# Rwkv slots of twelve steps: another placing of the features, the norm and the readout

## The chip, the cores and the metric

The kernel runs on one core of one Trainium2 chip. The metric is the device time of one execution in microseconds. The kernel before takes 4650.03 us (median of three runs, 4646.21 to 4650.68).

## The reference

Two transformer-like blocks of depth 2 run one after the other on 512 tokens of width 1024 (with 256 context tokens). Nearly all of it is left alone here. The change lies in the rwkv mixer of the first block: features are made from the projected keys, a decay and a rate; a linear recurrence over the tokens runs in both directions; and the outcome is normalised, gated and projected.

```python
kk = kk * lax.rsqrt(jnp.maximum(jnp.sum(kk * kk, axis=-1, keepdims=True), 1e-24))
decay = jnp.exp(-jnp.exp(-jax.nn.softplus(-w_raw) - 0.5))
a = jax.nn.sigmoid(heads(a0[d] + (xa @ a1[d]) @ a2[d]))
k_d = kh * (1 + (a - 1) * k_a_h)
...
S = (S * w_t[:, :, None, :]
     - jnp.einsum('bhij,bhj->bhi', S, kk_t)[..., None] * kka_t[:, :, None, :]
     + v_t[..., None] * k_t[:, :, None, :])
...
yn = ((y - mean) * lax.rsqrt(var + GN_EPS)).reshape(B, L, D_MODEL) * ln_g + ln_b
bonus = (jnp.sum(r * k_sum * r_k.astype(jnp.float32), axis=-1, keepdims=True) * v).reshape(B, L, D_MODEL)
return ((yn + bonus) * g).astype(dtype) @ wo
```

## The kernel before

Every engine runs its own instruction list. Each of these lists is made by the same Python walk, `rwkv_steps`, which calls `prep`, `scan`, `feature` and `readout` of that engine in one order. An engine does its list strictly in that order and waits on semaphores. So the tables that the change touches set the order in all five lists at once.

The sixteen heads are worked on as eight pairs. The 768 tokens of a pair are 12 chunks of 64, in three groups of four chunks, and each group of a pair is one slot: 24 slots in all, of 12 steps each (`PREP_STEPS`), t = 0 to 23. Slot t prepares its group in both directions (d = 0 and 1), and beside it the recurrence `scan` of the group of slot t - 1 runs, one part at every step: four chunks by three parts.

The preparation inverts a triangular matrix by levels. Step 0 makes the small and the big grams (PE L1722, L1732; the masked copy L3526 on VectorE and the products with a mask L3536 or L3538). Steps 2 to 9 are four levels of two steps: at an even step PE makes a product (L1782) and VectorE copies it under a mask (`copy_predicated`, L3544); at the odd step PE makes two (L1795, L1799) and ScalarE copies both (L2418). Step 10 is PE L1786 and the two ScalarE copies L2425, step 11 is PE L1810 and the two VectorE copies L3552. Each of these waits for the one before, and the two directions take turns. GpSimd sets the target of each masked copy to the unit matrix ahead of it (L1144).

`scan` has a product from the state (PE L1823) and VectorE L3570 in part 0, PE L1833 and the ScalarE copies L2439 in part 1, and PE L1845, L1852 and L1857 with VectorE L3577, L3579 and L3585 or L3589 in part 2.

The features of the *next* pair are made in the slots of this one, by `FEATURES[t % 3]`: a step's features are issued behind that step's `prep` and `scan`. `norm` of the pair *after* that is placed by `NORM_AHEAD` in the third slot. The readout of the pair *before* stands in the second slot by `READOUT` (not changed), its parts `turn` and `bonus` by `AHEAD` in the third. What each issues:

- lora: PE L1866 and ScalarE L2461 (Sigmoid), two each. recip: VectorE L3601, 128 columns of six. kk: L3603. run: a scan on VectorE, L3609. rate_k: ScalarE L2465 (Identity). key and rate: VectorE L3613, L3615.
- exp(d,0) and exp(d,1): ScalarE L2472, L2474 (Exp). exp(1,0) waits for kr(0,2), and kr(d,...) for exp(d,0). kr: VectorE L3624 to L3634; k_sum: L3637; bk: L3648; bonus: L3639.
- square: ScalarE L2449. norm: PE L1873 and VectorE L3596. root: ScalarE L2453 (Sqrt), behind norm.
- readout: centre (PE L1879), squares (ScalarE L2485), var (PE L1892, VectorE L3667), root (ScalarE L2488, Sqrt), recip0 to recip3 (VectorE L3673), scale, shift (L3676, L3679), gate (PE L1895, VectorE L3683), turn (PE L1884, ScalarE L2482), bonus (PE L1888, VectorE L3663).

Sigmoid, Exp and Sqrt each want their own table on ScalarE; a load stands in the list wherever one of them follows another. Copy, Identity and Square go with any. Two PSUM banks are used in turn by the small grams, the turned blocks, lora, norm and the readout (`misc_banks`), in the order of this same walk.

Of the kernel before, what the change touches and what calls it, by code (L numbers as in the profile page):

```python
# [294 lines left out]
def build_program(nc, panels, vecs, consts, x_in, c_in, mem_in, pool_w, bias, pos, window_in, out, x_save):  # L295
    npanels = panels.shape[0]
    with ExitStack() as ctx:
        def sb(name, shape, dt=F32):
            return ctx.enter_context(nc.sbuf_tensor(name, shape, dt))
# [13 lines left out]
        square = sb("square", [P, 2, TOK])  # L313
# [9 lines left out]
        def area(at, *shape):  # L323
            n = int(np.prod(shape))
            flat = arena[:, at:at + n]
            if len(shape) == 1:
                return flat
            names = " ".join("abcd"[:len(shape)])
            return flat.rearrange(f"p ({names}) -> p {names}", **{"abcd"[i]: s for i, s in enumerate(shape)})
# [297 lines left out]
        k_sum = area(RING0 + LORA_SLOT * PANEL + 3 * D, LAT)  # L627
# [15 lines left out]
        bk = [area(Y0 + d * 2 * BLOCK, CHUNKS // 2, 4, C) for d in range(2)]  # L643
# [116 lines left out]
        def ys(group):  # L760
# [6 lines left out]
        SCAN_AT = tuple(range(PREP_STEPS))  # L767
        RECIPS = 6
        FEATURES = (
            {0: [("recip", 0, 0)], 1: [("recip", 0, 1)], 2: [("recip", 0, 2)], 3: [("recip", 0, 3), ("lora", 0, 0)],  # L770
             4: [("recip", 0, 4)], 5: [("lora", 1, 0), ("recip", 0, 5)], 6: [("kk", 0, 0)], 7: [("run", 0, 0)],
             8: [("run", 0, 1)], 9: [("lora", 0, 1), ("run", 0, 2)], 10: [("lora", 1, 1), ("run", 1, 0)]},
            {0: [("run", 1, 1)], 1: [("rate_k", 0, 0), ("run", 1, 2)], 2: [("key", 0, 0)],
             3: [("rate_k", 1, 0), ("rate", 0, 0)], 5: [("exp", 0, 0)], 7: [("exp", 0, 1)]},
            {0: [("kr", 0, 0)], 1: [("kr", 0, 1), ("kr", 0, 2), ("exp", 1, 0)], 2: [("key", 1, 0)], 3: [("rate", 1, 0), ("exp", 1, 1)],
             4: [("kr", 1, 0)], 5: [("kr", 1, 1), ("kr", 1, 2), ("k_sum", 0, 0)], 6: [("bk", 0, 0)], 7: [("bk", 0, 1)],
             8: [("bk", 1, 0)], 9: [("bk", 1, 1)], 10: [("bonus", 0, 0)]})
        NORM_AHEAD = {9: "square", 10: "norm", 11: "root"}
        EARLY = [("square", 0, 0), ("norm", 0, 0), ("root", 0, 0), ("lora", 0, 0), ("lora", 1, 0), ("lora", 0, 1), ("lora", 1, 1)]
        EARLY += [("recip", 0, i) for i in range(RECIPS)] + [("rate_k", 0, 0), ("rate_k", 1, 0), ("kk", 0, 0)]  # L780
        EARLY += [("run", d, i) for d in range(2) for i in range(3)] + [("exp", 0, 0), ("exp", 0, 1)]
# [1 line left out]
        LATE = [("kr", 0, 0), ("kr", 0, 1), ("kr", 0, 2), ("bk", 0, 0), ("bk", 0, 1), ("exp", 1, 0), ("exp", 1, 1), ("kr", 1, 0), ("kr", 1, 1),  # L783
                ("kr", 1, 2), ("bk", 1, 0), ("bk", 1, 1), ("bonus", 0, 0)]

        AHEAD = {9: "turn", 10: "bonus"}
        READOUT = {1: ("centre",), 3: ("squares",), 4: ("var",), 5: ("root",), 6: ("recip0",), 7: ("recip1",), 8: ("recip2",),
                   9: ("recip3",), 10: ("scale", "shift"), 11: ("gate",)}

        def rwkv_steps(e):  # L790
# [9 lines left out]
            for t in range(groups + 1):  # L800
                for k in range(PREP_STEPS):
# [9 lines left out]
                    for what, d, i in FEATURES[t % GROUPS].get(k, ()):  # L811
                        if t // GROUPS + 1 < PAIRS:
                            e["feature"](t // GROUPS + 1, what, d, i)
                    if t % GROUPS == 2 and k in NORM_AHEAD and t // GROUPS + 2 < PAIRS:
                        e["feature"](t // GROUPS + 2, NORM_AHEAD[k], 0, 0)
                    if t % GROUPS == 1 and t > GROUPS and k in READOUT:
                        for what in READOUT[k]:
                            e["readout"](t // GROUPS - 1, what)
                    if t % GROUPS == 2 and k in AHEAD:
                        e["readout"](t // GROUPS, AHEAD[k])  # L820
            for k in sorted(READOUT):
# [3001 lines left out]
```

## Time and profile before

| | before |
|---|---|
| median of three runs | 4650.03 us |
| lowest, highest | 4646.21, 4650.68 us |
| the profiled execution | 4651.23 us, its span 4649.4 us |
| granted TensorE clock, mean | 0.974 |
| rwkv loop | about 1338 to 2000 us of the span |

The page gives the busy time of each engine over the whole span; the table of stretches gives it for a stretch, with the granted clock as a share of 2.4 GHz. A timeline row is the start, the length, the engine, the line and the operation, and in brackets the time that the engine sat idle before it with what ended that.

### The profile page before, as it was taken

To read this page: it belongs to the slowest core of one execution; us is meant where nothing else is said; L and a number is where in the kernel's file an instruction comes from. 1 tells how busy PE (TensorE), PEld (TensorE's weight loads), DVE (VectorE), ACT (ScalarE), POOL (GpSimd) and SP (SyncE) were. 2 spreads that over 40 slices of the span, in tenths; PEclk is the share of its full clock that TensorE was granted. 3 is DMA by queue.
4 is the path that set the end of the run, shared out by engine and by line. 5 is a ranking of instruction groups with operands and counts; after the bars stand their busy time and mean duration, and the time that the engine had idled before them with its cause. 6 is when DMAs were issued, how large, how long until landed. Compare 5 with 4: busy or idle time off the path is not lost.

```text
span 4649.4 us, 75968 instructions
## 1 busy us (share of the span) xinstructions
PE 4431.9 (95%) x32488; PEld 3163.7 (68%) x32488; DVE 2738.7 (59%) x4988; ACT 1042.5 (22%) x2236; POOL 243.0 (5%) x317
## 2 busy tenths in 40 slices
PE   8999999999988888899999999989999999989998
PEld 4555555556456666668886888547886888546887
DVE  3164545536358777645565666665657666674657
ACT  1053000012046666530002110341001010251000
POOL 0001000001001112110000000300000000110000
PEclk9999999999999999999999999989999999989999
DMA  5310222211200000122222222211222222201221
GB/s 210 146 63 37 91 109 109 109 55 57 84 2 3 4 4 4 39 83 73 91 91 76 90 74 82 91 37 73 91 86 86 77 86 82 91 37 73 91 91 46
DMA packets 27071, 339.45 MB, mean 73 GB/s; under 512 B 3025, under 2 KB 3025, under 8 KB 6897
## 3 DMA queue, kind: packets, MB, share of 16 engines
q1 hardware_dynamic: 24048, 324.51, 18.4%
q0 software_dynamic: 2688, 10.09, 0.6%
q8 instruction: 258, 4.23, 0.4%
q14 instruction: 77, 0.62, 0.0%
HBM read 330.40 MB, written 4.19 MB: 72 GB/s over the span
## 4 chain that ended last, share of the span: by engine, by line
PE 86%; DVE 8%; ACT 3%; issue 2%; DMA 1%; SPq 0%; DVEq 0%; ACTq 0%
PE ps L1583 47%; PE ps L1200 20%; PE ps L1209 2%; PE ps L1732 1%; PE ps L1795 1%; PE ps L1354 1%; PE ps L1253 1%; PE ps L1799 1%; PE ps L1516 1%; PE ps L1845 1%; ACT arena L2171 1%; PE ps L1866 1%; DVE arena L3536 1%; DMA arena<-in_panels 1%; PE ps L1662 1%
## 5 line engine op out<-in xcount | busy, mean ns | idle before, releaser
L1583 PE MATMUL ps<-arena 128*128 128x256 f32 (+1 forms) x9096 | 2108.6, 394 | 15.6 <-DVE arena L3199 15.6
L1583 PEld LDWEIGHTS ps<-arena 128*128 128x128 f32 x9096 | 1729.6, 190 | 381.7 <-DVE arena L3199 18.0
L1200 PE MATMUL ps<-arena 128*128 128x512 f32 (+3 forms) x2816 | 997.9, 515 | 0.4 <-DVE arena L2780 0.4
L1200 PEld LDWEIGHTS ps<-arena 128*128 128x128 f32 x2816 | 524.2, 190 | 460.1 <-issue 396.7
L3190 DVE TENSOR_TENSOR arena<-ps,arena 128x512 f32<-128x512 f32 (+1 forms) x250 | 157.6, 630 | 306.4 <-PE ps L1583 304.5
L3190 DVE TENSOR_TENSOR square<-ps,square 128x512 f32<-128x512 f32 (+1 forms) x145 | 99.1, 684 | 176.1 <-PE ps L1583 176.0
L3131 DVE TENSOR_TENSOR arena<-arena 128x1024 f32<-128x1024 f32 (+2 forms) x153 | 190.5, 1245 | 3.3
L2342 ACT COPY square<-ps 128x512 f32<-128x512 f32 (+1 forms) x65 | 37.2, 573 | 655.8 <-PE ps L1583 583.1
L1077 POOL TENSOR_TENSOR arena<-arena 128x512 f32<-128x512 f32 x60 | 72.0, 1200 | 1473.2 <-ACT arena L2142 1466.6
L2342 ACT COPY arena<-ps 128x384 f32<-128x384 f32 (+1 forms) x35 | 18.6, 530 | 572.3 <-PE ps L1583 546.5
L2418 ACT COPY arena<-ps 128x512 f32<-128x512 f32 x192 | 112.1, 585 | 99.7 <-PE ps L1799 95.6
L1144 POOL COPY square<-const 128x256 f32<-128x256 f32 x144 | 90.8, 638 | 725.4 <-PE ps L1799 497.0
L3199 DVE TENSOR_TENSOR arena<-arena 128x1024 f32<-128x1024 f32 (+1 forms) x60 | 72.4, 1207 | 87.2 <-ACT square L2342 78.4
L2171 ACT ACTIVATE arena<-arena,state_sum 128x256 f32<-128x256 f32 (+2 forms) x128 | 76.5, 598 | 207.0 <-DVE state_sum L2760 204.7
L3190 DVE TENSOR_TENSOR reset<-ps,square 128x512 f32<-128x512 f32 (+1 forms) x65 | 43.9, 675 | 132.7 <-PE ps L1583 132.7
L1583 PE MATMUL ps<-arena,square 128*128 128x256 f32 (+1 forms) x432 | 122.0, 431 | 0.0
L1209 PE MATMUL ps<-arena 128*128 128x256 f32 (+1 forms) x336 | 106.2, 478 | 15.1 <-DVE arena L2965 8.4
L1782 PE MATMUL ps<-arena 64*64 64x64 f32 x3072 | 91.3, 230 | 25.9 <-ACT arena L2418 20.3
L2333 ACT ACTIVATE reset<-arena 128x256 f32<-128x256 f32 x40 | 16.7, 417 | 422.7 <-DVE arena L3264 422.7
L3186 DVE TENSOR_TENSOR arena<-arena 128x1024 f32<-128x1024 f32 (+2 forms) x100 | 107.6, 1076 | 3.4
L3205 DVE TENSOR_TENSOR arena<-arena 128x1024 f32<-128x1024 f32 (+2 forms) x100 | 107.0, 1070 | 1.1
L1583 PEld LDWEIGHTS ps<-arena,square 128*128 128x128 f32 x432 | 82.1, 190 | 33.3
(392 smaller groups left out, 5201.1 us busy)
## 6 DMA issues: line engine op xcount, KB each, us to landing
arena<-in_panels SPq DMA_DIRECT2D x144, 2048.0 KB, 7.8
arena<-in_panels SPq DMA_DIRECT2D x9, 1536.0 KB, 6.4
arena<-in_bias POOLq DMA_DIRECT2D x8, 512.0 KB, 4.3
arena<-in_x_in SPq DMA_DIRECT2D x1, 3072.0 KB, 10.9
x_save<-arena POOLq DMA_DIRECT2D x1, 2048.0 KB, 7.5
arena<-x_save POOLq DMA_DIRECT2D x1, 2048.0 KB, 14.1
out_x<-arena SPq DMA_DIRECT2D x8, 256.0 KB, 2.9
arena<-in_panels SPq DMA_DIRECT2D x1, 1792.0 KB, 11.7
```

The costliest lines, as they stand in the source:

```text
L1144: pool.tensor_copy(step_sb[d][level % 2], unit).then_inc(sem("step_unit"), one("step_unit"))
L1200: ins = pe.matmul(dest, left(k), right(k), start=(k == 0), stop=(k == nk - 1))
L1209: ins = pe.matmul(bank[:, 0:b - a], w[:, k, m * P:(m + 1) * P], src[:, k, a:b], start=(k == 0), stop=(k == KD - 1))
L1583: ins = pe.matmul(bank[:, j * cut.side:(j + 1) * cut.side], left[:, k, j * P:(j + 1) * P], right[k], start=(k == 0), stop=(k == cut.rows - 1))
L1782: ins = pe.matmul(ps[half(home(level, h, pos)), 2 * d + pos, q * C:(q + 1) * C], left[half(pos), :], right[half(pos), :], start=True, stop ...
L2171: act.activation(p_h, p_h, ACT.Exp, bias=soft_at(i, h, NEGMAX), scale=-1.0, accum_out=soft_at(i, h, SUM)).then_inc(sem(f"exped{h}"), one(f ...
L2418: act.copy(both_sb[par][d], both_banks(d)[:, :, P:3 * P].rearrange("p a (w x) -> p a w x", w=2)).then_inc(sem(f"x_ready{d}"), one(f"x_read ...
L3131: ins = dve.tensor_tensor(part, x[:, rows], y[:, rows], op)
L3186: dve.tensor_tensor(a21, left_block(w, 0, 0, c), a21, ALU.subtract).then_inc(sem("left"), one("left"))
L3190: dve.tensor_tensor(out, product_of(tile(), cut), other, ALU.add).then_inc(sem("tile_free"), one("tile_free"))
L3199: dve.tensor_tensor(a11, left_block(total, 0, 0, cut), a11, ALU.subtract).then_inc(sem("tile_free"), one("tile_free"))
L3205: dve.tensor_tensor(a12, a12, a11, ALU.subtract).then_inc(sem("left"), one("left"))
```

## The change

Three tables change; no instruction is added, taken away or made otherwise, except the table loads, which follow the order of ScalarE's functions.

- First slot of a pair: recips 3 to 5 and kk at steps 4 and 6, lora(0,1) and lora(1,1) at steps 7 and 9 (were 9 and 10), run by run one step earlier or later.
- Second slot: rate from step 3 to 4, rate_k(1) from 3 to 9, exp(0,0) from 5 to 7, exp(0,1) from 7 to 9.
- Third slot: exp(1,0) from step 1 to 3, exp(1,1) from 3 to 5, k_sum from 5 to 6. Square, norm and root from steps 9, 10, 11 to 7, 8, 9. The readout's turn from 9 to 5, its bonus from 10 to 11.

```diff
         FEATURES = (
-            {0: [("recip", 0, 0)], 1: [("recip", 0, 1)], 2: [("recip", 0, 2)], 3: [("recip", 0, 3), ("lora", 0, 0)],
-             4: [("recip", 0, 4)], 5: [("lora", 1, 0), ("recip", 0, 5)], 6: [("kk", 0, 0)], 7: [("run", 0, 0)],
-             8: [("run", 0, 1)], 9: [("lora", 0, 1), ("run", 0, 2)], 10: [("lora", 1, 1), ("run", 1, 0)]},
-            {0: [("run", 1, 1)], 1: [("rate_k", 0, 0), ("run", 1, 2)], 2: [("key", 0, 0)],
-             3: [("rate_k", 1, 0), ("rate", 0, 0)], 5: [("exp", 0, 0)], 7: [("exp", 0, 1)]},
-            {0: [("kr", 0, 0)], 1: [("kr", 0, 1), ("kr", 0, 2), ("exp", 1, 0)], 2: [("key", 1, 0)], 3: [("rate", 1, 0), ("exp", 1, 1)],
-             4: [("kr", 1, 0)], 5: [("kr", 1, 1), ("kr", 1, 2), ("k_sum", 0, 0)], 6: [("bk", 0, 0)], 7: [("bk", 0, 1)],
+            {0: [("recip", 0, 0)], 1: [("recip", 0, 1)], 2: [("recip", 0, 2)], 3: [("lora", 0, 0)],
+             4: [("recip", 0, 3), ("recip", 0, 4)], 5: [("lora", 1, 0)], 6: [("recip", 0, 5), ("kk", 0, 0)], 7: [("lora", 0, 1)],
+             8: [("run", 0, 0), ("run", 0, 1)], 9: [("lora", 1, 1), ("run", 0, 2)], 10: [("run", 1, 0)]},
+            {0: [("run", 1, 1)], 1: [("rate_k", 0, 0), ("run", 1, 2)], 2: [("key", 0, 0)], 4: [("rate", 0, 0)],
+             7: [("exp", 0, 0)], 9: [("exp", 0, 1), ("rate_k", 1, 0)]},
+            {0: [("kr", 0, 0)], 1: [("kr", 0, 1), ("kr", 0, 2)], 2: [("key", 1, 0)], 3: [("exp", 1, 0), ("rate", 1, 0)],
+             4: [("kr", 1, 0)], 5: [("exp", 1, 1), ("kr", 1, 1), ("kr", 1, 2)], 6: [("k_sum", 0, 0), ("bk", 0, 0)], 7: [("bk", 0, 1)],
              8: [("bk", 1, 0)], 9: [("bk", 1, 1)], 10: [("bonus", 0, 0)]})
-        NORM_AHEAD = {9: "square", 10: "norm", 11: "root"}
+        NORM_AHEAD = {7: "square", 8: "norm", 9: "root"}
...
-        AHEAD = {9: "turn", 10: "bonus"}
+        AHEAD = {5: "turn", 11: "bonus"}
         READOUT = {1: ("centre",), 3: ("squares",), 4: ("var",), 5: ("root",), 6: ("recip0",), 7: ("recip1",), 8: ("recip2",),
                    9: ("recip3",), 10: ("scale", "shift"), 11: ("gate",)}
```

## Rows read from the trace of the kernel before

**Rows 1.** The page: busy time, share of the span and instructions of an engine.

```profile
PE 4431.9 (95%) x32488; PEld 3163.7 (68%) x32488; DVE 2738.7 (59%) x4988; ACT 1042.5 (22%) x2236; POOL 243.0 (5%) x317
```

**Rows 2.** The table of stretches: slots 10, 11, 12 and 22 of the loop.

```profile
core 0: us, PE busy (x) PEld busy (x) DVE busy (x) ACT busy (x) POOL busy (x), PEclk, DMA share, GB/s
...
1612.00:1643.80 31.80, 25.37 (x662) 18.65 (x662) 21.46 (x46) 22.47 (x46) 3.89 (x8) 0.87 0.01 3
1643.80:1671.40 27.60, 24.92 (x736) 19.93 (x736) 24.01 (x59) 15.80 (x36) 6.80 (x8) 0.96 0.02 4
1671.40:1696.40 25.00, 23.13 (x722) 18.08 (x722) 18.93 (x43) 17.21 (x41) 4.69 (x8) 1.00 0.01 3
...
1944.00:1974.40 30.40, 26.77 (x674) 20.06 (x674) 18.41 (x41) 15.65 (x38) 3.22 (x8) 0.85 0.01 3
```

**Rows 3.** Groups of ScalarE by line, 1338 to 2000: busy us, mean ns, idle before.

```profile
L2488 ACT ACT_TABLE_LOAD x7 | 9.0, 1283 | 0.1
L2474 ACT ACT_TABLE_LOAD x6 | 7.7, 1283 | 0.1
```

**Rows 4.** Timeline of ScalarE, slot 10: start, length, line, operation.

```profile
1623.78 1.03 ACT L2465 ACTIVATE arena<-arena,omka,vec 128x768 f32<-128x768 f32 x1
...
1628.81 1.28 ACT L2472 ACT_TABLE_LOAD   x1
1630.11 0.84 ACT L2472 ACTIVATE arena<-arena 128x768 f32<-128x768 f32 x1
1630.97 1.28 ACT L2488 ACT_TABLE_LOAD   x1
1632.26 0.63 ACT L2488 ACTIVATE rstd<-rstd 128x512 f32<-128x512 f32 x1
1632.80 0.57 ACT L2418 COPY arena<-ps 128x512 f32<-128x512 f32 x1
```

**Rows 5.** Timeline of TensorE, slot 10; in brackets its idle time before.

```profile
1625.38 1.13 PE L1892 MATMUL ps<-square,const 128*128 128x512 f32 x2 [0.98 <-ACT square L2485]
...
1633.42 0.46 PE L1782 MATMUL ps<-arena 64*64 64x64 f32 x16 [2.77 <-ACT arena L2418]
...
1640.55 2.08 PE L1895 MATMUL ps<-arena 128*128 128x512 f32 x2
```

**Rows 6.** The table of stretches, four us each, from slot 10 into 11.

```profile
1630.00:1634.00 4.00, 1.13 (x50) 0.85 (x50) 1.04 (x2) 3.92 (x8) 0.68 (x2) 1.00 0.00 0
1634.00:1638.00 4.00, 3.49 (x118) 3.04 (x120) 3.90 (x8) 3.40 (x5) 0.77 (x2) 0.72 0.02 4
...
1642.00:1646.00 4.00, 4.00 (x41) 3.10 (x41) 1.39 (x3) 0.37 (x1) 0.00 (x0) 0.50 0.00 0
1646.00:1650.00 4.00, 3.86 (x100) 3.13 (x99) 3.74 (x9) 1.73 (x6) 0.00 (x0) 1.00 0.02 4
```

**Rows 7.** Timeline of TensorE, slots 11 and 12.

```profile
1665.87 1.87 PE L1873 MATMUL ps<-square,const 128*128 128x384 f32 x4
...
1668.55 0.44 PE L1810 MATMUL ps<-arena 32*32 32x32 f32 x16
...
1691.17 0.92 PE L1866 MATMUL ps<-arena 64*128 64x384 f32 x4
```

**Rows 8.** Timeline of ScalarE, end of slot 11.

```profile
1666.73 0.53 ACT L2425 COPY arena<-ps 32x128 f32<-32x128 f32 x2
...
1668.38 1.28 ACT L2453 ACT_TABLE_LOAD   x1
```

**Rows 9.** Timeline of VectorE, slot 11, steps 5 to 8.

```profile
1658.74 0.68 DVE L3637 TENSOR_TENSOR arena<-arena 128x512 f32<-128x512 f32 x1
...
1662.27 0.43 DVE L3544 COPY_PREDICATED square<-const,ps 128x256 f32<-128x256 int32 x1
```

**Rows 10.** Timeline of TensorE, slot 22, which has a readout and no features.

```profile
1971.76 1.12 PE L1895 MATMUL ps<-arena 128*128 128x512 f32 x2
```

## What was predicted

> **What bounds the kernel now.** I read the page first. TensorE (PE) is busy 95% of the span and ScalarE (ACT) 22% [rows 1], but that is a mean over unlike stages. The change touches only the rwkv loop, about 1338 to 2000 us, so I cut that loop into its slots, taking the first masked copy of a slot (L3526) as its start. The table of stretches shows four slots of one kind each: a second slot of a pair with readout (31.8 us), a third (27.6), a first (25.0), and the last second slot, which has a readout but no features of a next pair (30.4) [rows 2]. No engine is full in the long one: PE 25.4, DVE 21.5, ACT 22.5 of 31.8 us [rows 2]. What sets its length is a ring: a product on PE, a masked copy on VectorE (DVE, L3544), a product, a copy on ACT (L2418), with the second direction half a step behind. A feature costs only what it adds to the queue ahead of the next ring instruction on its engine. So I follow each queue, in order of time, for one pair (slots 10, 11 and 12).
>
> **Second slot of a pair (31.8 us now).** Three ScalarE pieces stand in the ring.
> - Step 3: the rate_k activation (1.03 us) stands ahead of the readout's squares [rows 4], and PE waits 0.98 us for these before it starts the variance sum L1892 [rows 5]. The new table moves rate_k of direction 1 to step 9. PE is then free some 0.15 us before the squares end: 0.8 us won.
> - Step 5: a table load and exp(0,0), then another load and the readout's root, stand between two ring copies, from 1628.81 to 1632.89 [rows 4]; PE's next product waits 2.77 us [rows 5]. exp(0,0) goes to step 7, so 1.28 + 0.84 = 2.1 us leave this place. The recip pieces behind the root start as much earlier. In all L2418 would start near 1629.9 instead of 1632.80: 2.9 won.
> - Step 7: exp(0,0) with its load, 2.1 us, replaces exp(0,1), which has a load too [rows 3] and works on as many elements: nothing.
> - Step 9: exp(0,1) (0.84) and rate_k (1.03) now stand between the last L2418 and the first L2425, 1.9 us where nothing stood. PE has only its two small L1786 products and one L1833 to do meanwhile, and then waits about 1.8 us. Given back: 1.4 (the rest is the 0.3 to 0.5 us that L2425 was late anyway).
> - The variance read and rate on DVE: rate moves from step 3 to 4, into a wait; nothing.
> - The gate product L1895 takes 2.08 us here [rows 5] and 1.12 in the slot without features [rows 10]: the granted clock falls between 1634 and 1638, is 0.50 (1.2 GHz) until 1646 and then full again [rows 6]. With full clock the products of steps 9 to 11 win some 1.5 us together.
> Sum: -2.9 + 1.4 - 1.5 = **-3.0 us** if the clock stays full, -1.5 if it is half again by the gate product.
> The loads: L2488 and L2474 have their own load in each such slot [rows 3]; one of three loads goes in six slots, 6 x 1.28 = 7.7 us of ScalarE time. That is already in the 2.1 above. The Trainium skill (ScalarE: Activation LUTs, "What ACT_TABLE_LOAD costs") counts about 2.66 us for each switch, a drain included, and asks to group by set; here a load begins 0.02 us after the activation before it ends (1630.95) and its own activation follows 0.01 us behind it [rows 4], so no drain is to be seen and the sum goes by 1.28. By the page's figure the six would be 16 us.
>
> **Third slot (27.6 us now).**
> - k_sum (0.68 us) leaves step 5, where it holds up the masked copies of step 6 [rows 9], but stands at step 6 with bk(0,0), and bk(0,1) follows at step 7 as before. The copy of step 8, at 1662.27 [rows 9], comes when all of them are done, as now. Won at step 6, lost at step 8: 0.
> - exp(1,0) and exp(1,1) go to steps 3 and 5, each into a gap of ScalarE: 0. The turn (four transposes and a copy) at step 5 also falls in waits.
> - norm: four products L1873, 1.87 us [rows 7], move from step 10 to 8, ahead of L1795 of step 9. DVE releases the second direction's product only some 1.3 us later than the first's, so part is covered: +1.5.
> - root: load 1.28 + 0.84 = 2.1 us goes from step 11 [rows 8], where it hid under PE's queue, to step 9, ahead of L2425. The two squares and the turn's copy that stood there (1.7 us) leave: +0.4.
> - Step 10: the norm and bonus products that PE had there kept L1810 back to 1668.55 [rows 7], 1.3 us past the end of the copies it needs (L2425, 1667.26 [rows 8]); that goes: -1.3. But the copies L2439 and the second L2425 that this covered now follow in the open: +0.4.
> - The readout's bonus product L1888 at step 11 (about 1.05 us, by the like product L1895 at full clock [rows 10]) stands right ahead of the next slot: +1.05.
> Sum: **+2.1 us** (bounds +1.0, if the norm products hide behind the DVE queue, to +2.9, if nothing is covered).
>
> **First slot (25.0 us now).** The recips 3 to 5 and kk move between gaps of DVE; at most 0.2. The lora pair that ran at step 10, where ScalarE's copies covered most of it, now goes to step 7, ahead of L1782 of step 8: four L1866, 0.92 us [rows 7]. **+0.65 us** (bounds +0.2 and +0.9).
>
> **The rest.** Seventh first slot +0.65; slot 1, which has no readout to separate exp from exp, gets the 1.9 us of step 9: +1.5; slots 20 and 23 get the bonus at step 11: +0.5 each. Together +3.2.
>
> **The clock.** In the pair that I follow it falls once: in 1630 to 1634 PE is busy 1.13 of 4 us, and then the clock is 0.50 for some 10 us [rows 6]. The new table takes that hole away, but opens two others, of 1.8 us at step 10 of the second slot and of 2.1 us at step 10 of the third, with hardly any product around them: by my walk PE is busy some 1.2 of 3.5 us in each. That is about the share after which it fell [rows 6]. Right behind each hole comes the densest stretch, the gate or bonus product and the first products of the next slot, which is bound by PE. Half clock over some 3.5 us there costs about 1.5 us each time, by 2.08 against 1.12 for one product [rows 5, 10]. As the second slot's own end at half clock is the present state, the first costs back the 1.5 counted above; the second comes on top.
> The likeliest sum, for six pairs: 6 x (-3.0 + 2.1 + 0.65 + 1.5 + 1.5) = 6 x 2.75 = 16.5, and with the rest 19.7. Since the half clock may spare a seam now and then I take 18. The profiled execution is 4651.2 us (span 4649.4), 1.2 above the median of 4650.0, so 4650 + 18 = **4668 us**.
>
> **Rivals.**
> - **It is faster: the clock stays full.** Mechanism: the hole behind ScalarE's pair of loads (2.77 us) was the cause, and holes of about 2 us at step 10 don't suffice. Then the third slot also starts at full clock, which saves 1.1 us more, and if the norm products hide as well (+1.0): 6 x (-3.0 - 1.1 + 1.0 + 0.65) + 3.2 = -11.5: 4638. With norm as walked: 6 x (-1.35) + 3.2 = -5: 4645. It decides at a PE wait at step 10 of under about 1 us. For it: in the slot without features the same steps have no hole and stay at full clock. Against: 1.9 and 2.1 us of ScalarE work stand there without cover.
> - **Half clock at one of the two seams**, 6 x 1.25 + 3.2 = +11: 4661; if the other gains run 0.5 us better for each pair, +8: 4658.
> - **Half clock for longer than one such stretch.** Now it lasts about 10 us, not 3.5; two of these in a pair cost another 1 us each: +30: 4680.
> - **The change does nothing**: ring waits absorb the moves, the table load saved is not on the path: 4650. Against: the 2.77 us wait ends with that copy [rows 5].
>
> **Chances.** Forecast (both seams) 0.33, longer half clock 0.11, one seam 0.2 (0.09 of it above 0.2%), full clock 0.3 (0.2 of it below 4640.7, as the other terms of the walk have room on that side too), nothing 0.06. About 0.2%, 9.3 us, is what a measurement of this kernel can tell from no change. So faster 0.2, slower 0.33 + 0.11 + 0.09 = 0.53, same the rest, 0.27. The range takes in the full-clock case with its low bound and the longer half clock: 4636 to 4684.
>
> **What would show it.** Six loads fewer in all (L2474 without any). L2418 of step 7 some 2.9 us earlier in second slots. PE waits of 1.5 to 2.2 us for L2425 at step 10 of second and third slots. Second slots near 28.7 to 30.2 us, third ones near 29.7 to 31, first ones 25.7 (27 with half clock). The granted clock at 0.50 around the starts of slots and no longer before them. Wrong if the third slot is no longer than now: then the norm and root moves are covered by something that I don't see.

## The result, and the profile after

The changed kernel takes 4692.81 us (median, 4678.03 to 4694.34), the kernel before 4648.12 us beside it: a ratio of 1.0091 with the 95% interval 1.0068 to 1.0114. The forecast had the side (slower) and two of the three places where the clock falls, but it said 4668 us and a range up to 4684: the loss is more than twice what it gave.

The page after, engines and clock, to be laid beside [rows 1]:

```profile
PE 4463.4 (95%) x32488; PEld 3187.3 (68%) x32488; DVE 2740.2 (58%) x4988; ACT 1036.7 (22%) x2230; POOL 222.8 (5%) x317
...
PEclk9999999999998888899999999989999999989999
```

TensorE is busy 31.5 us longer with the same 32488 products, and five slices of the clock's line, those of the rwkv loop, have gone from 9 to 8. ScalarE issues six instructions fewer: the six table loads. The span is 4691.6 us, 42.2 more than before. The table of stretches, first for the whole loop and then for the slots 10, 11, 12 and 22 (as [rows 2]; columns as there):

```profile
1343.90:2019.30 675.40, 588.01 (x15942) 453.76 (x15941) 469.84 (x1071) 400.53 (x892) 92.26 (x184) 0.87 0.03 9
...
1633.60:1665.70 32.10, 26.82 (x660) 19.75 (x662) 21.43 (x45) 20.49 (x44) 3.30 (x8) 0.82 0.01 3
1665.70:1696.10 30.40, 26.42 (x728) 20.43 (x728) 23.84 (x59) 17.47 (x39) 5.05 (x8) 0.89 0.01 4
1696.10:1725.90 29.80, 27.11 (x726) 21.55 (x728) 19.41 (x44) 16.57 (x38) 3.85 (x8) 0.84 0.01 3
1991.40:2019.30 27.90, 24.13 (x660) 17.17 (x661) 18.53 (x41) 15.87 (x39) 3.20 (x8) 0.94 0.01 3
```

and the same loop, 23 slot lengths, in the kernel before:

```profile
1343.20:1974.40 631.20, 553.15 (x15956) 428.75 (x15953) 468.82 (x1071) 406.31 (x898) 112.36 (x184) 0.93 0.03 10
```

The loop has grown by 44.2 us, which is all of the loss. VectorE's busy time is the same (468.8 and 469.8), ScalarE's is less (406.3 and 400.5). What grew is TensorE's, by 35 us, and its clock went from 0.93 to 0.87. A share of 0.87 over 675.4 us is 2 x 0.13 x 675.4 = 176 us at half clock, against 2 x 0.07 x 631.2 = 88 us before. So there are 88 us more at half clock and 44 us more of time. This quotient, a half, is no price yet, as it also holds what the queues gained and lost; the first experiment gives about 0.4 us of time for each microsecond at half clock. Slot 22, with no features in it, is 2.5 us shorter than before, at a clock of 0.94 instead of 0.85.

The second slot is as long as before (32.1 against 31.8), the third is 2.8 us longer, the first 4.8 us. The two waits that the forecast spoke of, on TensorE (timeline; the idle time before it in brackets), slots 10 and 11:

```profile
1660.66 0.51 PE L1810 MATMUL ps<-arena 32*32 32x32 f32 x16 [1.84 <-ACT arena L2425]
...
1661.84 0.64 PE L1810 MATMUL ps<-arena 32*32 32x32 f32 x16
1662.41 2.08 PE L1895 MATMUL ps<-arena 128*128 128x512 f32 x2
...
1665.46 2.08 PE L1732 MATMUL ps<-arena 64*128 64x128 f32 x16
...
1690.51 0.44 PE L1810 MATMUL ps<-arena 32*32 32x32 f32 x16 [2.25 <-ACT arena L2425]
...
1692.32 0.64 PE L1810 MATMUL ps<-arena 32*32 32x32 f32 x16
1692.88 2.08 PE L1888 MATMUL ps<-arena,const 128*128 128x512 f32 x2
...
1695.94 1.97 PE L1732 MATMUL ps<-arena 64*128 64x64 f32 x16
```

And what ScalarE did meanwhile:

```profile
1658.30 0.85 ACT L2474 ACTIVATE arena<-arena 128x768 f32<-128x768 f32 x1
1659.04 1.02 ACT L2465 ACTIVATE arena<-arena,omka,vec 128x768 f32<-128x768 f32 x1
1660.08 0.53 ACT L2425 COPY arena<-ps 32x128 f32<-32x128 f32 x2
...
1687.77 1.28 ACT L2453 ACT_TABLE_LOAD   x1
1689.07 0.84 ACT L2453 ACTIVATE rstd<-rstd 128x768 f32<-128x768 f32 x1
1689.93 0.53 ACT L2425 COPY arena<-ps 32x128 f32<-32x128 f32 x2
```

The two waits are there, of 1.84 and 2.25 us (walked, that is, followed queue by queue in the prediction: 1.8 and 2.1), each ended by L2425 behind two pieces of ScalarE work. Right behind each the products run at half speed: L1895 and L1888 take 2.08 us instead of 1.12 [rows 10]. The clock over these stretches:

```profile
1658.40:1661.00 2.60, 0.76 (x40) 0.58 (x36) 2.13 (x3) 2.53 (x7) 0.00 (x0) 0.98 0.02 6
1661.00:1665.00 4.00, 3.95 (x43) 2.13 (x40) 2.21 (x7) 2.89 (x9) 0.00 (x0) 0.50 0.00 0
1665.00:1668.50 3.50, 3.50 (x53) 3.09 (x50) 1.56 (x4) 0.00 (x0) 0.00 (x0) 0.61 0.00 0
...
1688.00:1692.00 4.00, 1.63 (x55) 1.33 (x56) 2.03 (x6) 3.44 (x8) 0.00 (x0) 0.95 0.00 0
1692.00:1696.00 4.00, 4.00 (x44) 2.20 (x40) 1.81 (x5) 2.23 (x6) 0.00 (x0) 0.50 0.02 4
1696.00:1700.00 4.00, 4.00 (x48) 3.77 (x48) 1.89 (x5) 0.00 (x0) 0.00 (x0) 0.50 0.00 0
1700.00:1704.00 4.00, 4.00 (x67) 3.11 (x69) 2.57 (x4) 1.53 (x5) 0.00 (x0) 0.50 0.00 0
1704.00:1708.00 4.00, 4.00 (x114) 3.29 (x113) 2.43 (x6) 1.60 (x4) 0.03 (x1) 0.84 0.02 4
...
1722.00:1726.00 4.00, 2.93 (x90) 2.40 (x88) 2.28 (x8) 3.47 (x12) 0.00 (x0) 0.97 0.00 0
1726.00:1730.00 4.00, 2.47 (x30) 2.18 (x30) 1.74 (x4) 1.07 (x3) 0.00 (x0) 0.50 0.01 4
1730.00:1734.00 4.00, 4.00 (x60) 3.25 (x56) 1.93 (x4) 0.76 (x3) 0.00 (x0) 0.68 0.00 0
```

The clock falls at the end of the second slot, of the third, and of the first one too (in what follows, at three seams): about 7, 13.5 and 7 us of half clock, 27 in a pair, where it was about 10 [rows 6]. In the third slot's case it lasts through the whole dense start of the next slot. The experiments ask whether the clock is the cause or only goes with it.

### The profile page after: what moved, and what is told of

The parts are those of the page before. It is cut to its first block, busy times and chain, and to the rows that moved or that the text cites. A ratio compares the mean times of both kernels' runs of the same rounds, so it can differ in the third digit from the quotient of the medians.

```text
span 4691.6 us, 75966 instructions
## 1 busy us (share of the span) xinstructions
PE 4463.4 (95%) x32488; PEld 3187.3 (68%) x32488; DVE 2740.2 (58%) x4988; ACT 1036.7 (22%) x2230; POOL 222.8 (5%) x317
## 4 chain that ended last, share of the span: by engine, by line
PE 86%; DVE 7%; ACT 4%; issue 2%; DMA 1%; SPq 0%; DVEq 0%; ACTq 0%
PE ps L1583 46%; PE ps L1200 20%; PE ps L1209 2%; PE ps L1732 2%; PE ps L1354 1%; PE ps L1795 1%; PE ps L1253 1%; PE ps L1722 1%; ACT arena L2171 1%; PE ps L1516 1%; PE ps L1845 1%; PE ps L1799 1%; ACT arena L2418 1%; DVE arena L3536 1%; DMA arena<-in_panels 1%
## 5 line engine op out<-in xcount | busy, mean ns | idle before, releaser
L2418 ACT COPY arena<-ps 128x512 f32<-128x512 f32 x192 | 111.7, 584 | 82.8 <-PE ps L1799 77.5
L1144 POOL COPY square<-const 128x256 f32<-128x256 f32 x144 | 75.5, 526 | 791.0 <-PE ps L1799 562.0
L1583 PEld LDWEIGHTS ps<-arena,square 128*128 128x128 f32 x432 | 82.1, 190 | 33.3
L2705 DVE SCALAR_TENSOR_TENSOR arena<-arena,vec 128x512 f32<-128x512 f32 x120 | 103.4, 902 | 1.3
```

Of the source, the lines that this page charges most:

```text
L1144: pool.tensor_copy(step_sb[d][level % 2], unit).then_inc(sem("step_unit"), one("step_unit"))
L1583: ins = pe.matmul(bank[:, j * cut.side:(j + 1) * cut.side], left[:, k, j * P:(j + 1) * P], right[k], start=(k == 0), stop=(k == cut.rows - 1))
L2418: act.copy(both_sb[par][d], both_banks(d)[:, :, P:3 * P].rearrange("p a (w x) -> p a w x", w=2)).then_inc(sem(f"x_ready{d}"), one(f"x_read ...
L2705: ins = dve.scalar_tensor_tensor(conv_y[:, c, :], src, w, conv_y[:, c, :], ALU.mult, ALU.add)
```

## Experiments

**Does the clock carry the loss?** The changed kernel, with products on TensorE that nobody reads, put into its waits at the start of step 11. They go to the PSUM bank that is free there, behind the wait that frees it.

```diff
+                elif k in (11,) and d == 0:
+                    b = len(plan) % 2
+                    plan[("hold", t, k)] = (4 + b, last[b])
...
+                if k in (11,) and d == 0:
+                    bank = misc("hold", t, k)
+                    for _ in range(8):
+                        pe.matmul(ps[:, bank, 0:P], ident, ident, start=True, stop=True)
```

> The changed kernel with eight products of 128 columns that nobody reads put on TensorE at the start of step 11 of every slot, where it sits waiting (about 1.4 us of work in waits of 1.8 to 2.2 us); nothing else differs. Theory 1 (the granted clock, which falls after the waits at step 10, carries most of the loss): the clock is at 0.50 for under 5 us in a pair instead of 27, the three slots take 28.7, 29.7 and 25.8 us instead of 32.0, 30.5 and 29.8, and the kernel 4645 us (4637 to 4655). Theory 2 (the loss is the longer queues of ScalarE and VectorE and the norm products themselves): the slots stay within 0.3 us of the changed kernel's or grow, 4690 to 4700 us.

Measured: 4642.54 us, ratio to the kernel before 0.9992 (0.9982 to 1.0001), 50 us less than the changed kernel by doing more work. The slots of one pair (second, third, first) take 28.0, 27.6 and 26.5 us. The end of slot 10, TensorE's timeline, and then the loop and the stretch around that seam:

```profile
1632.84 2.05 PE L1720 MATMUL ps<-const 128*128 128x128 f32 x16
1634.82 0.44 PE L1817 MATMUL ps<-arena 32*32 32x32 f32 x16
1635.31 0.45 PE L1852 MATMUL ps<-arena 128*64 128x64 f32 x8
1635.85 0.44 PE L1817 MATMUL ps<-arena 32*32 32x32 f32 x16
1636.22 1.12 PE L1902 MATMUL ps<-arena 128*128 128x512 f32 x2
```

```profile
1344.90:1965.80 620.90, 563.72 (x16312) 446.18 (x16310) 468.09 (x1070) 400.41 (x892) 93.23 (x184) 0.99 0.03 10
...
1634.00:1638.00 4.00, 3.86 (x68) 2.62 (x68) 3.03 (x8) 3.82 (x13) 0.00 (x0) 1.00 0.00 0
```

(Its lines are 7 further down: L1902 is the gate product, L1817 is L1810.) The fillers take 2.05 us, not the 1.4 that the expectation gave, so they stick out a little, and the first slot pays 0.8 us for them; yet the gate product is back at 1.12 us and the loop is at full clock, 0.99. Theory 2, the queues alone, is out: all ScalarE and VectorE queues are as in the changed kernel, and the loss is gone. The three slots take 82.1 us together instead of 92.3, with none of the 27 us of half clock left: 10.2 / 27, or 0.38 us for each, and 0.41 if the 0.8 us of the fillers is counted in.

Half as many fillers:

> The changed kernel with four unread products at step 11 instead of eight (0.7 us of work in waits of 1.8 to 2.2). If the clock falls after a stretch with too little work in it, four are near the bound: it stays full at some seams and falls at others, half clock 5 to 15 us in a pair, 4650 to 4670 us. If each product only hides in its wait and the clock is no matter: 4692.

4640.71 us, 0.9990 (0.9981 to 0.9999). Better than expected. The clock holds behind nearly all second slots and falls for 3 to 7 us behind most third ones, some 33 us in the loop. Four (about 1 us) buy nearly as much clock as eight and cost the first slot less (25.9 us).

Is it that they fill the *wait*, or would products anywhere do? The same eight at step 3:

> The changed kernel with the same eight unread products, but at the start of step 3 of every slot, where TensorE does not wait long; the waits of step 10 stay open. Theory 1 (the clock falls because of the thin stretch at steps 10 and 11, so the place matters): the clock falls as in the changed kernel, about 170 us of half clock in the loop, and the products add 1.0 to 1.4 us to each of 24 slots: 4715 to 4730 us. Theory 2 (more products anywhere raise the mean activity and keep the clock up): under 60 us of half clock, 4650 to 4680.

```diff
-                elif k in (11,) and d == 0:
+                elif k in (3,) and d == 0:
...
-                if k in (11,) and d == 0:
+                if k in (3,) and d == 0:
```

4721.87 us, 1.0161 (1.0144 to 1.0178): in the expected band, 29 us above the changed kernel. The clock over its loop is 0.91, some 126 us of half clock (expected: 170, and 176 without the products). So the place decides most of it: at step 11 the same eight leave next to nothing of the half clock, at step 3 they take away some 50 us, which theory 1 had not foreseen, and cost more than that brings.

**The same in the kernel before.** Its own fall came behind the 2.77 us wait of step 8 [rows 5, 6].

```diff
+                elif k in (8,) and d == 0 and t % GROUPS == 1:
+                    b = len(plan) % 2
+                    plan[("hold", t, k)] = (4 + b, last[b])
...
+                if k in (8,) and d == 0 and g == 1:
+                    bank = misc("hold", t, k)
+                    for _ in range(12):
+                        pe.matmul(ps[:, bank, 0:P], ident, ident, start=True, stop=True)
```

> The kernel before with twelve products of 128 columns that nobody reads on TensorE at the start of step 8 of every second slot, in the wait of 2.77 us there. Theory 1 (clock): it no longer falls in the second slot; second slot 30.1 us, third 26.6: 4631 us (4624 to 4638). Theory 2 (queues alone): 4647, or longer by what sticks out of the wait.

4639.88 us, 0.9989 (0.9980 to 0.9998). The direction is as theory 1 has it, the size is not: 7 us, not 16. The clock over the loop is 0.97 instead of 0.93, so some 50 us less at half clock, and the loop is 8.9 us shorter: under 0.2 us for each here. The second slot is 30.5 us. Twelve products are over 3 us long by the 2.05 for eight, more than the wait, and TensorE also waits in that slot for other reasons; how much of the missing gain is which was not measured.

**Which part of the change makes the waits?** Each of the kernel before with one part.

Second slot's table alone:

```diff
-             3: [("rate_k", 1, 0), ("rate", 0, 0)], 5: [("exp", 0, 0)], 7: [("exp", 0, 1)]},
+            {0: [("run", 1, 1)], 1: [("rate_k", 0, 0), ("run", 1, 2)], 2: [("key", 0, 0)], 4: [("rate", 0, 0)],
+             7: [("exp", 0, 0)], 9: [("exp", 0, 1), ("rate_k", 1, 0)]},
```

> The kernel before with only the second slot's table changed (exp at steps 7 and 9, rate_k at 9, rate at 4). Theory 1 (clock): the 2.8 us wait of step 7 goes and one of about 1.9 us at step 10 comes, the clock still falls once in a pair, later and for some 7 us; second slot 29.7 us, third 27.6: 4637 us (4630 to 4645). Theory 2 (queues alone): 2.9 us less and 1.4 more, 1.5 in each pair: 4641. If the seam behind it gets longer than now: 4650.

4640.51 us, 0.9985 (0.9976 to 0.9994), second slot 29.7 us: faster, as both theories said, which differ too little here to be told apart.

First slot's table alone:

```diff
-             8: [("run", 0, 1)], 9: [("lora", 0, 1), ("run", 0, 2)], 10: [("lora", 1, 1), ("run", 1, 0)]},
+             8: [("run", 0, 0), ("run", 0, 1)], 9: [("lora", 1, 1), ("run", 0, 2)], 10: [("run", 1, 0)]},
```

(with the lora and recip moves of steps 3 to 7 as in the change)

> The kernel before with only the first slot's table changed (the last lora pair from steps 9 and 10 to 7 and 9, recips by two). Theory 1 (clock): without the lora products at step 10 the stretch at the end of the first slot is thin, the clock falls in some pairs and the second slot starts 2.3 us longer: first slot 25.7, kernel 4662 us (4654 to 4672). Theory 2 (queues alone): 0.6 us in each pair: 4653 to 4655.

4656.92 us, 1.0015 (1.0006 to 1.0025). The first slot is 25.7 us, 0.6 more, and the second behind it 32.7 instead of 31.7, as the clock falls at the end of the first. That is 10 us from a table whose own queues cost 4: theory 1.

The norm part alone:

```diff
-        NORM_AHEAD = {9: "square", 10: "norm", 11: "root"}
+        NORM_AHEAD = {7: "square", 8: "norm", 9: "root"}
```

> The kernel before with only square, norm and root put at steps 7, 8, 9 of the third slot. Theory 1 (clock): the third slot grows by 1.5 to 2 us, TensorE waits over 1 us for the last ScalarE copies at step 10, and the clock falls behind it for some 13 us, so that the first slot grows by 4 us too: 4683 us (4670 to 4690). Theory 2 (queues alone): only the 1.5 to 2 us of the third slot: 4660 us (4657 to 4664).

4680.99 us, 1.0061 (1.0038 to 1.0085): theory 1. Its third slots take 29.2 us on average and its first ones 29.4 instead of 25.1, though nothing of a first slot was changed.

The rest, the third slot's features with turn and bonus:

```diff
-        AHEAD = {9: "turn", 10: "bonus"}
+        AHEAD = {5: "turn", 11: "bonus"}
```

(with exp(1,.) at 3 and 5 and k_sum at 6)

> The kernel before with the third slot's features (exp(1,.) at 3 and 5, k_sum at 6) and with turn at 5 and bonus at 11; norm and root as before. Theory 1 (walk): what k_sum wins at step 6 is lost at step 8, the bonus product uncovered at step 11 costs up to 0.5 us, no new wait of TensorE, clock as before: third slot 27.6 to 28.1 us, 4650 us (4645 to 4653). Rival (at most two long VectorE features between masked copies does shorten the slot): 26.9 us, 4643.

4645.27 us, 1.0000 (0.9990 to 1.0009): no difference in time, as theory 1 had it. The third slot did shorten by 0.9 us in its profile (26.3 against 27.2), so that the rival's reason has something. Why the median doesn't show it can be read in part: the profile is of an execution of 4640.46 us, below its own median, and that of the kernel before is of one of 4651.23, above its own, with more half clock in its loop (0.93 against 0.96). Between third slots that have no half clock at all the gain is 0.7 us (26.0 against 26.7), and the first slots take 25.5 instead of 25.1. What is left, some 2 us in six pairs, is within the interval.

**And of the norm part, which instruction?** The changed kernel with the root alone put back:

```diff
-        NORM_AHEAD = {7: "square", 8: "norm", 9: "root"}
+        NORM_AHEAD = {7: "square", 8: "norm", 11: "root"}
```

> The changed kernel with only the root of the norm put back to step 11; square and norm stay at 7 and 8. The wait for the root's table load and activation ahead of the L2425 copies in the third slot goes (2.1 us), the 1.5 us of the norm products at step 8 stay. Theory 1 (walk and clock): third slot 28 to 28.5 us instead of 30.5, first slot 26 to 27.5 instead of 29.8, second as changed at 32 or, with less half clock behind it, 30: 4662 us (4650 to 4670). Theory 2 (queues alone): 2.1 us in each of six: 4680.

4645.93 us, 1.0000 (0.9990 to 1.0009). One ScalarE table load and one activation, at step 9 instead of 11 in six slots, cost 47 us for 6 x 2.12 = 12.7 us of work; the rest of the change gains about as much as it loses. This is below the range of theory 1 (4650 to 4670), in its direction, and far from the 4680 of the queues alone. The third slot falls from 30.5 to 26.7 us and the first from 29.7 to 25.9. The slots 10, 11 and 12:

```profile
1615.80:1645.40 29.60, 24.25 (x662) 17.45 (x660) 21.41 (x45) 20.59 (x44) 3.30 (x8) 0.93 0.02 3
1645.40:1672.00 26.60, 24.78 (x729) 19.68 (x728) 23.47 (x59) 15.65 (x35) 5.07 (x8) 0.95 0.02 4
1672.00:1697.70 25.70, 23.01 (x728) 18.13 (x725) 19.23 (x44) 18.02 (x43) 3.86 (x8) 1.00 0.01 3
```

The wait behind the second slot's ScalarE pieces is still there, and so is its fall; the fall behind the third slot is gone, and in this pair the one behind the first, too. The clock over the loop is 0.93 again, 88 us of half clock less than in the changed kernel. The loop is 46.2 us shorter; without the 12.7 us of work itself that leaves 33.5 us, again some 0.4 us for each (an estimate, as it takes the work to have been waited for in full).

**Without waits, and without fillers.** The changed kernel with rate_k, exp(0,1) and the norm part out of the way:

```diff
-             7: [("exp", 0, 0)], 9: [("exp", 0, 1), ("rate_k", 1, 0)]},
-            {0: [("kr", 0, 0)], 1: [("kr", 0, 1), ("kr", 0, 2)], 2: [("key", 1, 0)], 3: [("exp", 1, 0), ("rate", 1, 0)],
+             7: [("exp", 0, 0)], 11: [("rate_k", 1, 0)]},
+            {0: [("kr", 0, 0)], 1: [("exp", 0, 1), ("kr", 0, 1), ("kr", 0, 2)], 2: [("key", 1, 0)], 3: [("exp", 1, 0), ("rate", 1, 0)],
...
-        NORM_AHEAD = {7: "square", 8: "norm", 9: "root"}
+        NORM_AHEAD = {9: "square", 10: "norm", 11: "root"}
```

> The changed kernel without the two waits and without fillers: rate_k(1) at step 11 and exp(0,1) at step 1 of the third slot, square, norm and root back at 9, 10, 11; all else as changed (first slot, k_sum at 6, turn at 5, bonus at 11). Theory 1 (walk and clock): second slot 28 to 29 us, third 26.5, first 25.7; the clock falls only at the end of some first slots: 4630 us (4622 to 4642). If it is the first slot's table or the bonus at step 11 that makes the clock fall: over 4650.

4633.99 us, 0.9974 (0.9965 to 0.9983), as expected, though the second slot takes 29.6 us and not 28 to 29. The clock over its loop is still 0.93: it keeps falling at the end of the first slots, as in the run with the first slot's table alone.

**The version that beats both.** So the first slot is left as it was before, too, and the readout's bonus stays at step 10:

```diff
-             3: [("rate_k", 1, 0), ("rate", 0, 0)], 5: [("exp", 0, 0)], 7: [("exp", 0, 1)]},
-            {0: [("kr", 0, 0)], 1: [("kr", 0, 1), ("kr", 0, 2), ("exp", 1, 0)], 2: [("key", 1, 0)], 3: [("rate", 1, 0), ("exp", 1, 1)],
-             4: [("kr", 1, 0)], 5: [("kr", 1, 1), ("kr", 1, 2), ("k_sum", 0, 0)], 6: [("bk", 0, 0)], 7: [("bk", 0, 1)],
-             8: [("bk", 1, 0)], 9: [("bk", 1, 1)], 10: [("bonus", 0, 0)]})
+            {0: [("run", 1, 1)], 1: [("rate_k", 0, 0), ("run", 1, 2)], 2: [("key", 0, 0)], 4: [("rate", 0, 0)],
+             7: [("exp", 0, 0)], 11: [("rate_k", 1, 0)]},
+            {0: [("kr", 0, 0)], 1: [("exp", 0, 1), ("kr", 0, 1), ("kr", 0, 2)], 2: [("key", 1, 0)], 3: [("exp", 1, 0), ("rate", 1, 0)],
+             4: [("kr", 1, 0)], 5: [("exp", 1, 1), ("kr", 1, 1), ("kr", 1, 2)], 6: [("bk", 0, 0)], 7: [("bk", 0, 1)],
+             8: [("bk", 1, 0)], 9: [("k_sum", 0, 0), ("bk", 1, 1)], 10: [("bonus", 0, 0)]})
...
-        AHEAD = {9: "turn", 10: "bonus"}
+        AHEAD = {5: "turn", 10: "bonus"}
```

> A fourth table, by the same walk: of the second slot only what won (exp(0,0) behind the readout's root, rate before step 5), rate_k(1) at step 11 and exp(0,1) at step 1 of the third slot, so that nothing stands ahead of the L2425 copies; exp(1,.) at steps 3 and 5, k_sum at step 9, turn at step 5, and norm, root, the readout's bonus and the whole first slot as before. Theory 1 (walk and clock): no TensorE wait of over 1.2 us is left in a slot, the clock stays full in most pairs, second slot 27.7 us, third 26, first 25.0: 4612 us (4603 to 4625). Theory 2 (queues alone, clock falls as before): second slot 29.5, third 27: 4629. Theory 3 (the readout's own load and root keep the clock falling once in a pair): 4625 to 4632.

4617.26 us, 0.9938 (0.9926 to 0.9951) of the kernel before, 29 us less. Its whole loop, then slots 10, 11 and 12:

```profile
1351.10:1944.00 592.90, 532.19 (x15956) 411.65 (x15954) 467.25 (x1071) 398.82 (x892) 104.74 (x184) 0.98 0.03 11
...
1607.10:1634.20 27.10, 23.41 (x674) 17.38 (x672) 21.21 (x45) 20.01 (x44) 3.29 (x8) 1.00 0.01 4
1634.20:1659.60 25.40, 23.14 (x724) 18.16 (x720) 23.86 (x60) 17.21 (x39) 5.72 (x8) 1.00 0.02 4
1659.60:1684.70 25.10, 23.23 (x722) 18.18 (x722) 18.93 (x43) 16.85 (x40) 4.59 (x8) 1.00 0.01 3
```

The clock is full in all three. The walk gave 27.7, 26 and 25.0 us for them and 4612 in all; over the five pairs of slots 4 to 18 they take 27.5, 26.1 and 25.1 on average. The loop is 38 us shorter than before, the kernel only 29 by its medians: the loop starts 7.9 us later here than in the profile before, which no run explains.

## Why the prediction was right, and where it was wrong

The step that failed is the term for the clock: half clock over 3.5 us at each of two seams. The runs show 7 us behind the second slot, 13.5 behind the third, and 7 behind the first, where the forecast had no fall at all. The waits and the queues came near. One by one:

- **The six loads.** Right: six ScalarE instructions fewer, none by L2474. What they were worth alone no run tells, as exp(0,1) and rate_k moved with them. The rows show no drain here either: the activation starts 0.02 us after its load ends (1689.07).
- **Second slot.** L2418 of step 7 comes 20.0 us after the slot's start, against 20.65 before; but the start itself, up to the first L2431, is 2.4 us longer by the half clock, so the queue's gain is 3.0 (walked: 2.9). The wait at step 10 is 1.84 us (walked: 1.8), and the slot is 32.0 us (walked: 30.2 with half clock at its end). Missing is the half clock at its *start*.
- **Third slot.** The wait is 2.25 us (2.1). Without the root this slot would not have grown: 26.7 us in the run with the root late, 0.5 less than before, where the walk's other terms sum to about 0. So the norm products at step 8 and the uncovered copies were priced a little too high, and the slot is 30.5 by the root and the clock.
- **First slot.** Its own queues: +0.6 (walked: +0.65, measured in the run with this table alone). It is 4.7 us longer in the changed kernel (forecast: 25.7 us, or 27 with half clock; measured 29.7), as the half clock of the seam ahead lasts through its start. Here the failed term weighs most.
- **The clock, the step that failed.** The forecast let the clock fall at two seams, by the share of busy time ahead of them, and there it falls. It gave 3.5 us of half clock to each, at 1.5 us of cost. The price for a microsecond (0.43) was near the measured 0.4; the durations were not, and the 3.5 us had no row behind them: the fall in the kernel before lasted 10 us [rows 6]. This stood in the forecast only as a rival, with 0.11 and 1 us more for each seam, where it should have been the base case. The third fall, behind the first slot, it had not at all: the walk had counted the moved lora products only as a queue, and the stretch ahead of that fall is busy 2.93 of 4 us, far more than the 1.2 of 3.5 that it reckoned with at the two others. In sum 27 us of half clock for a pair instead of 7, against 10 before.
- **An error the other way.** With the clock full, the walk gives 31.8 - 3.0 = 28.8, 27.6 + 2.1 - 1.1 = 28.6 and 25.65 us for the three slots, 83.1 together. The run with the fillers has 82.1 at full clock, the fillers' 0.8 us in it. So the queues were walked some 1.8 us too dear for a pair, and that hid part of the clock's error.
- **The rival "clock stays full"** has its number now: with the fillers 4642.54, near the 4645 that it gave. That it comes so near is partly luck, as the fillers' own time stands in the one and the queues' 1.8 us in the other. The rival failed on the clock: waits of 1.84 and 2.25 us were enough to make it fall.

The Trainium skill (TensorE: Matmul & The Clock Gate, "What's actually happening") says that the clock follows how busy the engine has been of late, and the trace agrees at the two waits: 0.76 of 2.6 us busy at full clock, then 0.50. The fall behind the first slot, after 2.93 of 4 us, shows that the share of busy time alone doesn't settle it.

What is not settled: what exactly makes the clock return after 7 us in one place and after 13.5 in another. Nor is it clear when the first slot's table makes it fall: in the run with the root late the same table stands at the end of every first slot, and in the four from slot 9 to 18 the clock doesn't fall there.

## What to carry to other kernels

Where TensorE is near its bound, price a wait by two terms: its own length, and the time at half clock behind it, here at some 0.4 us for each where TensorE is the bound, and less where it waits anyway (12.7 us of ScalarE work moved into such a place cost 47 us). So put the work of the other engines where TensorE has products to make, and least of all ahead of the last small products before a dense stretch. When activations are grouped to save a table load, look at where the group comes to stand. And a wait that can't be removed can be filled: products that nobody reads gave back the whole loss.

## What the runs showed of the hardware that was not expected

- The clock fell, too, behind a stretch with TensorE busy 2.93 of 4 us (1722 to 1726 in the changed kernel), where no wait was over 0.96 us and the products were small, with 32 or 64 columns. In the kernel before it stayed full through a stretch that was busy less, so the busy share alone doesn't tell when it falls:

```profile
1612.00:1616.00 4.00, 2.47 (x50) 2.21 (x50) 2.23 (x6) 1.80 (x5) 0.00 (x0) 1.00 0.00 0
1616.00:1620.00 4.00, 3.85 (x75) 2.37 (x74) 3.23 (x6) 2.83 (x7) 0.00 (x0) 1.00 0.03 6
```

- Once down it stayed so for 7 to 13.5 us, in the longest case with TensorE busy all of the time (1692 to 1704 in the changed kernel).
- Eight fp32 products of 128 x 128 by 128 columns took 2.05 us at full clock, each in two passes (x16), 0.13 us for each pass.
